# Differential attention on one core: zero-padded keys and one score product per head, with banks, values, exponentials and last splits reordered

## The reference, cut to what matters

```python
q = rope((x @ w_q).reshape(b, s, 8, 2, 64), angles) * 64 ** -0.5
for i in range(s // 128):                      # two tiles of 128 queries
    sc = einsum('bqhmd,bkhmd->bhmqk', qb, kb)  # two halves m of every head h
    mask = causal
    p = softmax(where(mask, sc, -inf), axis=-1)
    a = p[:, :, 0] - lam * p[:, :, 1]
    outs.append(einsum('bhqk,bkhe->bqhe', a, vb))
o = rms over each head's 128 values, times a gain
return o @ w_out
```

## Time and profile before

| what | value |
|---|---|
| median of three runs | 2356.43 us (2355.14 to 2358.28) |
| profiled execution, its span | 2356.36 us, 2354.5 us |
| TensorE matmul busy | 2322.8 us (99%), 12380 instructions |
| VectorE busy | 1708.0 us (73%) |
| ScalarE busy | 1322.9 us (56%) |
| GpSimd busy | 448.3 us (19%) |
| mean DMA rate | 174 GB/s |
| score products L936 | 64 records, from 1065.7 to 1139.1 us |
| value products L958 | 48 records, from 1115.9 to 1150.7 us |

### The profile page before, as it was taken

One profiled execution on the slowest core, in us unless ns is written; L12 is line 12 of the kernel. 1 busy time (PEld: TensorE's weight loads), 2 busy tenths in 40 slices (PEclk: granted clock), 3 DMA queues, 4 the chain that ended last, 5 costly groups with the idle time before them and its releaser, 6 DMA issues.

```text
span 2354.5 us, 33293 instructions
## 1 busy us (share of the span) xinstructions
PE 2322.8 (99%) x12380; PEld 1977.7 (84%) x12380; DVE 1708.0 (73%) x3088; ACT 1322.9 (56%) x2179; POOL 448.3 (19%) x348
## 2 busy tenths in 40 slices
PE   8999999999999999999899999999999999999999
PEld 8778888899988888877688888998888888877887
DVE  7466588888975555667748898898555665777885
ACT  3454555577664544545555557766454554666554
POOL 1000233177720000000014225774000000000000
PEclk9999999999999999999999999999999999999999
DMA  7455555544456666653345555444656666433555
GB/s 254 147 179 179 162 187 188 190 143 134 135 180 195 201 193 196 218 167 126 135 151 187 191 179 162 134 135 145 213 197 204 219 200 200 137 117 124 173 189 176
DMA packets 112096, 408.53 MB, mean 174 GB/s; under 512 B 12592, under 2 KB 12640, under 8 KB 111680
## 3 DMA queue, kind: packets, MB, share of 16 engines
q1 hardware_dynamic: 107712, 391.63, 50.9%
q0 software_dynamic: 3504, 13.47, 1.7%
q10 hardware_dynamic: 720, 1.31, 0.2%
HBM read 405.30 MB, written 1.05 MB: 173 GB/s over the span
## 4 chain that ended last, share of the span: by engine, by line
PE 87%; DVE 7%; ACT 3%; DMA 2%; issue 1%; ACTq 0%; DVEq 0%
PE ps L623 23%; PE ps L626 12%; PE ps L697 11%; PE ps L701 11%; PE ps L693 10%; PE ps L875 5%; PE ps L662 3%; PE ps L659 3%; PE ps L666 3%; DVE lo L1910 2%; DMA raw<-in_peer_v 1%; PE ps L752 1%; ACT hi L1332 1%; PE ps L609 1%; PE ps L612 1%; PE ps L606 1%
## 5 line engine op out<-in xcount | busy, mean ns | idle before, releaser
L1910 DVE TENSOR_TENSOR lo<-raw,hi 128x1024 fp32r<-128x1024 f32 (+1 forms) x627 | 767.7, 1228 | 386.5 <-ACT hi L1332 382.6
L1332 ACT ACTIVATE hi<-raw 128x1024 fp32r<-128x1024 f32 x677 | 714.5, 1057 | 510.8 <-PE ps L701 264.7
L623 PE MATMUL ps<-xs,hi 128*128 128x512 f32 x2560 | 651.1, 396 | 1.1 <-ACT hi L1332 1.1
L623 PEld LDWEIGHTS ps<-xs,hi 128*128 128x128 f32 x2560 | 459.6, 189 | 83.7 <-DVE big L2832 1.3
L626 PEld LDWEIGHTS ps<-xs,lo 128*128 128x128 f32 x2560 | 349.0, 190 | 26.1
L626 PE MATMUL ps<-xs,lo 128*128 128x256 f32 x2560 | 356.7, 282 | 0.0
L2909 POOL TENSOR_SCALAR lnp<-iota,selT 128x128 f32<-128x128 f32 x256 | 300.2, 1182 | 191.3 <-PE ps L875 102.4
L693 PE MATMUL ps<-hi,lefts 128*128 128x512 f32 x986 | 304.1, 390 | 1.7 <-ACT lefts L1369 1.7
L697 PE MATMUL ps<-hi,lefts 128*128 128x512 f32 x986 | 304.0, 390 | 0.9 <-DVE lefts L1976 0.9
L701 PE MATMUL ps<-lo,lefts 128*128 128x512 f32 x986 | 303.8, 389 | 0.0
L697 PEld LDWEIGHTS ps<-hi,lefts 128*128 128x128 f32 x986 | 184.8, 188 | 40.5 <-DVE lefts L1976 2.4
(11 more groups left out here) (373 smaller groups left out, 2546.1 us busy)
## 6 DMA issues: line engine op xcount, KB each, us to landing
raw<-in_peer_u SPq DMA_DIRECT2D x256, 512.0 KB, 3.3
raw<-in_peer_v SPq DMA_DIRECT2D x256, 512.0 KB, 4.2
raw<-in_ret_vg SPq DMA_DIRECT2D x32, 512.0 KB, 3.3
raw<-in_peer_q SPq DMA_DIRECT2D x24, 512.0 KB, 3.4
raw<-in_ffn_up SPq DMA_DIRECT2D x22, 512.0 KB, 3.3
raw<-in_ffn_down SPq DMA_DIRECT2D x22, 512.0 KB, 4.3
raw<-in_ffn_gate SPq DMA_DIRECT2D x18, 512.0 KB, 4.3
raw<-in_ret_qk SPq DMA_DIRECT2D x16, 512.0 KB, 4.5
```

What stands on the lines that cost most here:

```text
L623: e.matmul(out, uh[:, k, :], xs[:, k, :, :].rearrange("p h t -> p (h t)"), start=k == 0, stop=False)
L1332: e.activation(parts(i)[0][:, 0:w], raw[:, i % N_RAW, 0:w], ACT.Copy).then_inc(s_hi, 1)
L1910: e.tensor_tensor(ul[:, 0:w], raw[:, i % N_RAW, 0:w], uh[:, 0:w].bitcast(F32), ALU.subtract).then_inc(s_lo, 1)
```

## The change

- **Scores.** `Diff.kT` gives way to two padded key stores of two banks each: for half m = 0 the 64 rows of half 1 are zero, for m = 1 the rows of half 0. One fp32 product with 128 rows then gives both halves: 2 x 128 columns for qt 0, 512 columns for qt 1. `me.wait()` is gone. Heads 0 to 3 use a new `pad` (in the place of `kT`) and the front halves of `dk` and `dq`.
- **Reading out keys.** `keys_T` copies 64 rows twice where one copy took 128 rows: on ScalarE and on VectorE, at steps 0 and 7.
- **Zeros.** GpSimd issues six memsets, two of 64x1024 and four of 64x512, and TensorE waits for them (`s_pad`) at steps 2 and 10.
- **Banks.** Two banks of UPPER are skipped after the transposes of step 7 and of step 9; `dq0` is claimed after the four `diff_k0` units of tile 0 instead of before them.
- **Values.** `diff_added(1, 0)` comes after the first `out_half`.
- **Exponentials and transposes of the last items** move ahead on all three engines; `out_half(2, 1)` moves ahead of `diff_turn(0)`.
- **Last splits.** The split of `diff_turn(1)` comes ahead of the first `peer_q1` unit on ScalarE and VectorE; that unit's low part is made after the norm of tile 0.

```diff
-            dk0, dq0 = tok_claim("diff_k0", 0, ("dk", 0)), tok_claim("diff_q0", 0, ("dq", 0))
+            dk0 = tok_claim("diff_k0", 0, ("dk", 0))
             for s in range(4):
                 tok_unit("diff_k0", 0, dk0, s, 0, X_DIFF)
+            dq0 = tok_claim("diff_q0", 0, ("dq", 0))
...
-                        for m in range(2):
-                            rows = slice(m * 64, (m + 1) * 64)
-                            if m == 1:
-                                me.wait()
-                            ins = e.matmul(u.view[:, m * 256:m * 256 + kw], Diff.qT[rows, h, qt * 128:(qt + 1) * 128],
-                                           Diff.kT[rows, h, 0:kw], start=True, stop=True)
-                            if m == 0:
-                                me.did(ins)
-                        ins.then_inc(u.filled[0], 1)
+                        pads = Diff.pads[j][h % 4 // 2][:, :, h % 2 * 256:h % 2 * 256 + kw]
+                        e.matmul(u.view.rearrange("p (m k) -> p m k", m=2)[:, :, 0:kw],
+                                 Diff.qT[:, h, qt * 128:(qt + 1) * 128], pads, start=True, stop=True).then_inc(u.filled[0], 1)
...
                 if i == 7:
                     e.wait_ge(s_qk, 3)
                     diff_T("dkT", Diff.dk, 1)
+                    for _ in range(2):
+                        psum.skip(UPPER)
...
-            diff_added(1, 0)
             us = acc_claim("diff_w_out", 8)
...
             for k in range(2):
                 out_half(k, 0)
+                if k == 0:
+                    diff_added(1, 0)
                 out_half(k, 1).then_inc(s_used, 1)
-                if k == 0:
+                next(heads1)
+            for k in range(2, 8):
+                if k == 4:
                     next(heads1)
-            for k in range(2, 8):
-                if k in (3, 4):
-                    next(heads1)
-                if k == 4:
+                    out_half(2, 1).then_inc(s_used, 1)
                     diff_turn(0)
                     diff_added(1, 1)
...
+            def keys_T(j):
+                u = use[("dkT", j), 0]
+                e.wait_ge(*u.filled)
+                for m in range(2):
+                    rs = slice(m * 64, (m + 1) * 64)
+                    ins = e.tensor_copy(Diff.pads[j][0][rs, m, :], u.view[rs, :])
+                ins.then_inc(u.freed[0], 1)
...
+            e.wait_ge(s_used, used("peer_v0", 127))
+            for m in range(2):
+                e.memset(Diff.pad[64 - 64 * m:128 - 64 * m, m, :], 0.0).then_inc(s_pad, 1)
             e.wait_ge(s_norm, 8)
             ln_load(1, 0)
+            for i, place in enumerate((Diff.dk, Diff.dq)):
+                for b in range(2):
+                    e.wait_ge(*use[(("dkT", "dqT")[i], 0), b].filled)
+                for m in range(2):
+                    e.memset(place[64 - 64 * m:128 - 64 * m, m, 0:2 * S], 0.0).then_inc(s_pad, 1)
```

More of the change, by code:

```diff
@@ L301, in build @@
         s_oh, s_ol = sem("heads_hi_made"), sem("heads_lo_made")
+        s_pad = sem("padding_zeroed")
         s_ang, s_trig = sem("angles_ready"), sem("trig_ready")
@@ L449, in build @@
             R = region(big, 8704)
-            qT, kT = R(8, S), R(8, S)
+            qT, pad = R(8, S), R(2, 4 * S)
+            pads = [[pad[:, :, 0:2 * S], pad[:, :, 2 * S:4 * S]], [dk[:, :, 0:2 * S], dq[:, :, 0:2 * S]]]
             P = several(R, 2, 2, S)
@@ L972, in beside @@
                 if i == 2:
+                    e.wait_ge(s_pad, 2)
                     wait_T(("dkT", 0), 2)
@@ L982, in beside @@
                     diff_T("dqT", Diff.dq, 1)
+                    for _ in range(2):
+                        psum.skip(UPPER)
                 if i == 10:
+                    e.wait_ge(s_pad, 6)
                     wait_T(("dkT", 1), 2)
@@ L1033, in pe @@
             diff_turn(1)
-            for k in range(2, 8):
+            for k in range(3, 8):
                 out_half(k, 1).then_inc(s_used, 1)
@@ L1604, in act @@
             heads0, heads1 = diff_heads(0), diff_heads(1)
+            def keys_T(j):
+                u = use[("dkT", j), 1]
+                e.wait_ge(*u.filled)
+                for m in range(2):
+                    rs = slice(m * 64, (m + 1) * 64)
+                    ins = e.activation(Diff.pads[j][1][rs, m, :], u.view[rs, :], ACT.Copy)
+                ins.then_inc(u.freed[0], 1)
             def beside(i):
                 if i == 0:
-                    odd_T(("dkT", 0), Diff.kT[:, 0:4, :], 2)
+                    keys_T(0)
                 if i == 1:
@@ L1613, in beside @@
                 if i == 7:
-                    odd_T(("dkT", 1), Diff.kT[:, 4:8, :], 2)
+                    keys_T(1)
                 if i == 9:
@@ L1651, in act @@
             hi_to(n0 + 7)
+            diff_left(3, Diff.oh[:, 4:8, 128:256], lambda v: v.rearrange("p (k t) -> p k t", k=4))
             hi_to(W.first["peer_q1"])
-            diff_left(3, Diff.oh[:, 4:8, 128:256], lambda v: v.rearrange("p (k t) -> p k t", k=4))
             def square(src, dst, t):
@@ L2388, in dve, with keys_T @@
             heads0, heads1, steps0, steps1 = diff_heads(0), diff_heads(1), norm0(), (norm1(0), norm1(1))
+            def keys_T(j):
+                u = use[("dkT", j), 0]
+                e.wait_ge(*u.filled)
+                for m in range(2):
+                    rs = slice(m * 64, (m + 1) * 64)
+                    ins = e.tensor_copy(Diff.pads[j][0][rs, m, :], u.view[rs, :])
+                ins.then_inc(u.freed[0], 1)
             def beside(i):
                 if i == 0:
-                    even_T(("dkT", 0), Diff.kT[:, 0:4, :], 2)
+                    keys_T(0)
                 if i == 1:
@@ L2401, in beside @@
                 if i == 7:
-                    even_T(("dkT", 1), Diff.kT[:, 4:8, :], 2)
+                    keys_T(1)
                 if i == 8:
@@ L2417, in dve @@
             next(heads1)
-            lo_to(n0 + 2)
-            next(steps1[0])
             next(heads1)
@@ L2422, in dve @@
             next(heads1)
+            next(steps1[0])
             next(steps1[0])
@@ L2430, in dve @@
                     next(steps1[1])
-                    lo_to(W.first["peer_q1"])
+                    lo_to(n0 + 7)
                 diff_left(2 + t, Diff.ol[:, 4:8, t * 128:(t + 1) * 128], lambda v: v.rearrange("p (k t) -> p k t", k=4),
```

## The result

The changed kernel took 2341.85 us (median of 4 runs, 2341.29 to 2342.66) against 2356.47 us before: ratio 0.9936, 95% interval 0.9925 to 0.9948, so faster by 0.5 to 0.75%. The profiled execution took 2341.58 us, 14.78 less than the one before.

The account below looks back on a forecast made before the run. TensorE, busy 99% at full clock, was taken as the bound; 0.7 + 1.5 + 8.1 + 2.4 + 2.7 - 1.2 = 14.2 us off 2356.36 gave 2342.2 us, range 2339.0 to 2347.0.

Parts of the forecast that it names:

- Claim of `dq0`: First `diff_k0` product no longer held for the low split of its input: 0.7 us gained, bounds 0 and 0.75.
- Scores: Differential attention, steps 2 to 14: 13 scores each 0.62 us cheaper on the mean, 8.1 us gained.
- So a score costs 0.52 or 0.95: Price of the padded score product with 128 or 256 keys, including 0.09 for the change of kind: 0.64 or 0.59 less.
- Banks: Claims at steps 8 and 12 no longer wait 0.73 us each for read-outs: 1.5 us gained, bounds 0 and 1.5.
- `diff_w_out`: Scaled heads to last transposes: 22.8 us in place of 25.2, 2.4 us gained, bounds 0.5 and 3.5.
- Last splits: Last transposes to residual: 2.7 us gained; low part behind the norm, ahead of TensorE's awaited split: 1.2 us lost.
- Costed at nothing: VectorE 0.9 us behind from key copies, ScalarE's copies, GpSimd's memsets and SyncE's later fourth `peer_q1` issue: no cost.
- the gaps did not stay: Rival, score products: gaps around them stay, 3.8 us less gained, 2346.0 us; chance 0.10.
- the end came forward: Rival, end of attention: `peer_q1` transfers hold it, the last three terms (3.9 us) vanish, 2346.1 us; chance 0.17.
- signs of being wrong: Wide score 1.1 us or more; VectorE never idle, TensorE waiting; ScalarE waiting for DMA before root; clock under 1.00.
- VectorE did not become the bound: Rival, attention steps: VectorE, with 0.26 us slack, bounds them and half the scores' gain is lost, 2346.2 us; chance 0.12.
- The clock: Rival, 1153 to 1166 us: clock falls to 1.2 GHz; slower overall only at 38 us low; chance 0.02.

Follow-up runs that it names:

- the bench: A small kernel of TensorE products only, one score case at a time between groups of fp32r products: a padded product 0.885 us, 64-row halves with the wait 1.605.
- the read-out move: Changed kernel with ScalarE reading out turned queries of heads 4 to 7 ahead of step 9's exponentials; with tile 0 added to the residual before the last split, 2341.03 us.
- the scores alone: The kernel before with only the padded keys, memsets, split copies and the single score product: 2348.93 us.
- two moves more: Changed kernel with ScalarE's query read-out ahead of step 9's exponentials and the second `peer_q1` unit's low part on GpSimd: 2343.77 us.

## Why the prediction was right

2342.2 was forecast, 2341.85 came, and the terms hold one by one, that of the scores only since errors of opposite sign met. That the sum came so close is partly luck too.

- **Claim of `dq0`, 0.7:** 0.83, just over its upper bound of 0.75.
- **Scores, 8.1:** 8.13 at the scaled heads by putting the old products back (7.70 by the start of the 13th score). The 8.56 at the normed tile 1 holds also the 0.61 of head 7, which the prediction counted in `diff_w_out`. The price in "So a score costs 0.52 or 0.95" was too high: 0.44 and 0.87. I had kept 0.09 for the change of kind behind the product; on balance it isn't there. The saving is 0.72 and 0.67 instead of 0.64 and 0.59; against it a wait at step 10 and the wait ahead of the scaled heads (1.49 instead of the 1.2 expected) took part of it back. That both gaps belong to the 64-row form is shown by the bench: 0.09 ahead and 0.18 behind (0.29 expected), with 0.10 more inside.
- **Banks, 1.5:** 1.81, from undoing it. The waits of the claims would have been 0.95 and 0.73 beside the cheaper score.
- **`diff_w_out`, 2.4:** 2.72, the score of head 7 included. The wait of 0.6 expected at the first half showed as 0.21 and a slow start, the 0.7 at the last unit as 0.28.
- **Last splits, 2.7 and -1.2:** 2.67 and -1.14.
- **Costed at nothing:** here a step failed. VectorE's lateness was "0.9 behind" and free; it cost about half a us at step 10, by way of ScalarE, as the read-out move shows (0.53). The copies themselves took 0.69 us for 64 rows (two in 1.38, VectorE, 1083.71), as long as 128 rows, where 0.6 was assumed. And SyncE's later issue of the fourth `peer_q1` unit did not make TensorE wait, as counted; but GpSimd's low part of it moved beside VectorE's norm of tile 1, whose centring took 1.72 instead of 1.28 us: the 0.44 between the second pair and the normed tile 1. The prediction had no term for it, though it moved that low part itself.
- **The sum:** 14.2 forecast, 14.24 at the normed tile 1 and 14.78 between the profiled executions; the rest is scatter of what lies behind. Banks and scores together, 9.6 forecast, are 9.60 from the transposes of tile 1 to the scaled heads. Claim and `diff_w_out` came 0.13 and 0.32 above their terms, the uncounted slow centring 0.44 below: these errors cancel.
- **Rivals:** the gaps did not stay; the end came forward; of the signs of being wrong one showed, ScalarE waiting for a DMA ahead of the root (0.54 us for tile 0, 3.08 for tile 1), but it then waited for VectorE's input of the root 0.98 and 1.97 us longer, so the transfer didn't hold the root. It did set when GpSimd's low part began (1157.15), and so the 0.44 above. VectorE did not become the bound, though 3.4 us more on it would have cost 1.5. The clock stayed at its full level with waits of 1.49, 0.95 and 1.51 us, but fell in two neighbours of this kernel. The 0.02 I gave it was for a fall of 38 us; falls of 3 us, worth 1.5 us each where nothing covers them, are near.

The parts add up nearly: at the normed tile 1, 8.56 for the scores and 2.61, 2.68 and 0.97 for banks, order and last splits, undone one by one in the changed kernel, are 14.82 against 14.24. The score of head 7, 0.6, is counted with both the scores and the order, as only the new order lets it win; that is as much as the sum has too much. The other overlaps nearly cancel (0.35 too much already at the scaled heads, 0.4 too little behind the last transposes). The 8.74 of the scores alone is no part of this sum: it holds the 1.6 lost to the lower clock and 2.4 won at the last split, where the transfer had landed.

## What to carry to other kernels

Two products of 64 rows with a wait between them cost more than one of 128 with zeros: the form costs 0.37 us (0.27 to enter and leave, 0.10 inside), the wait 0.3. With a bank each and several pairs in a row the halves would run in parallel at half the price; that was measured on the bench, not built into the kernel. An engine with slack on average can still hold TensorE through a bank that a third engine reads out behind it; look at what stands ahead of each read-out. And work that a waiting engine could do with inputs that are already there (the residual, 1.99 us of idle ahead of it) is worth more than moving work to an idle engine beside it.

## What was not expected of the hardware

- VectorE's centring of 128x1024 (L2024, which reads `x`, `mv` and `lnp`) nearly stood still while GpSimd made a low part: 1.28 us alone, 1.72 with 0.63 us beside GpSimd (in the changed kernel), 2.52 with 1.45 and 2.68 with 1.61 us beside it (tile 0 and tile 1 of the run with two moves more). Each time it ended 1.07 to 1.09 us after GpSimd did, so only some 0.2 us of its work was done side by side. The statistics of the tile (L2018, which read `x` alone) ran beside GpSimd in the changed kernel and took their usual 1.27 us.
- The granted clock fell from 2.4 to 1.2 GHz for some 3 us behind TensorE waits of 0.83, 0.49 and 1.26 us in one profile, and not in another with the same waits; and behind one of 2.20 us. What decides between the first two stays open.
- The parallel run of 64-row tiles: 0.43 us for each further pair of products of 256 columns, against 0.895 for two padded ones, one behind the other.
